# Products with the rows of v issued for four gathers at a time

## The reference, cut to what matters

```python
def peer_ffn(x, w_q, sub_keys, u_emb, v_emb):
    ...
    def chunk(xc):                                    # 128 tokens
        q = (xc @ w_q).reshape(PEER_CHUNK, PEER_HEADS, 2, PEER_HALF)
        s = jnp.einsum('thid,hikd->thik', q, sub_keys).astype(jnp.float32)
        ...                                           # the best 16 of 16384 experts per head: eidx, gate
        u = u_emb[eidx]
        hid = jax.nn.gelu(jnp.einsum('td,thkd->thk', xc, u))
        wgt = (gate * hid.astype(jnp.float32)).astype(xc.dtype)
        return jnp.einsum('thk,thkd->td', wgt, v_emb[eidx])
```

## Time and profile before

| | us |
|---|---|
| median of three runs | 4032.74 (4027.02 to 4035.24) |
| profiled execution, its own time | 4030.91 |
| its span | 4029.6 |
| PE busy in the span | 3244.0 (81%) |
| DVE busy | 1976.9 (49%) |
| POOL busy | 1526.5 (38%) |
| line 1854, products with v, 3072 records | 1067.8 |
| line 2025, gathers, 1536 issues | 1456.6 |
| gathers' share of the DMA engines' span | 50.9% |

### The profile page before, as it was taken

One profiled execution on the slowest core, in us unless ns is written; L12 is line 12 of the kernel. 1 busy time (PEld: TensorE's weight loads), 2 busy tenths in 40 slices (PEclk: granted clock), 3 DMA queues, 4 the chain that ended last, 5 costly groups with the idle time before them and its releaser, 6 DMA issues.

```text
span 4029.6 us, 28457 instructions
## 1 busy us (share of the span) xinstructions
PE 3244.0 (81%) x10226; PEld 1353.4 (34%) x10226; DVE 1976.9 (49%) x4445; ACT 376.2 (9%) x923; POOL 1526.5 (38%) x1577
## 2 busy tenths in 40 slices
PE   7989978777898877788878888878666666788898
PEld 3464334622452222522222222344511111134444
DVE  0041034776776663766666623134777677414122
ACT  1000031111000000000000000032000000012112
POOL 0010000364665564376666641000377777700000
PEclk9999989878999998899999999999888899899999
DMA  4134333797999998799999985311899999952222
GB/s 190 63 126 154 150 122 125 309 346 276 394 412 405 409 394 324 304 412 411 411 412 411 412 338 229 147 65 66 327 402 409 409 408 397 409 204 84 106 104 94
DMA packets 257129, 1125.38 MB, mean 279 GB/s; under 512 B 29552, under 2 KB 34672, under 8 KB 237788
## 3 DMA queue, kind: packets, MB, share of 16 engines
q0 software_dynamic: 221184, 805.40, 50.9%
q1 hardware_dynamic: 32380, 312.82, 19.9%
q10 hardware_dynamic: 3424, 5.34, 0.4%
HBM read 1117.06 MB, written 6.40 MB: 279 GB/s over the span
## 4 chain that ended last, share of the span: by engine, by line
PE 47%; DMA 25%; DVE 14%; POOL 7%; issue 4%; ACT 2%; SPq 0%; DVEq 0%; ACTq 0%
PE ps L228 15%; DMA big<-in_u,xT 15%; DMA big<-in_v,xT 7%; POOL big L2025 7%; PE ps L1854 5%; DVE big L1994 5%; PE ps L587 4%; PE ps L342 4%; PE ps L1793 4%; PE ps L1294 2%; PE ps L1330 2%; DMA w<-in_w_in 1%; PE ps L599 1%; PE ps L527 1%; PE ps L749 1%
## 5 line engine op out<-in xcount | busy, mean ns | idle before, releaser
L1854 PE MATMUL ps<-big,bc 128*32 128x512 f32 x3072 | 1067.8, 668 | 336.6 <-DMA big<-in_v,xT 324.0
L1994 DVE CUSTOM_DVE_ANT_0 big<-big,ps 128x1024 f32<-128x1024 f32 x768 | 926.3, 1215 | 423.7 <-DMA big<-in_u,xT 420.1
L2025 POOL DMA_INDIRECT big<-in_u,xT x768 | 729.0, 949 | 625.8 <-issue 166.6
L2025 POOL DMA_INDIRECT big<-in_v,xT x768 | 727.6, 947 | 278.7 <-issue 186.5
L228 PE MATMUL ps<-w,xT 128*128 128x512 f32 x1408 | 613.0, 597 | 18.6 <-DMA w<-in_w_in 10.0
L1854 PEld LDWEIGHTS ps<-big,bc 128*32 128x32 f32 x3072 | 193.2, 115 | 1093.8 <-DMA big<-in_v,xT 727.6
L228 PEld LDWEIGHTS ps<-w,xT 128*128 128x128 f32 x1408 | 268.8, 192 | 357.3 <-issue 344.6
L467 POOL TENSOR_TENSOR small<-small 128x32 f32<-128x32 f32 (+1 forms) x8 | 33.2, 4154 | 480.1 <-DVE small L438 329.8
L342 PE MATMUL ps<-w,small 128*2 128x512 f32 x384 | 180.5, 626 | 41.3 <-DMA w<-in_w_mod 40.7
L587 PE MATMUL ps<-w,xT 128*128 128x512 f32 x384 | 173.0, 610 | 17.3 <-DMA w<-in_w_in 15.6
L876 POOL TENSOR_TENSOR small<-small 128x8 f32<-128x8 f32 x4 | 6.5, 1634 | 448.7 <-DVE small L867 448.7
(11 more groups left out here) (295 smaller groups left out, 3006.7 us busy)
## 6 DMA issues: line engine op xcount, KB each, us to landing
w<-in_w_in SPq DMA_DIRECT2D x58, 2048.0 KB, 7.7
w<-in_w_mod SPq DMA_DIRECT2D x24, 2048.0 KB, 7.4
w<-in_w_conv SPq DMA_DIRECT2D x24, 1536.0 KB, 9.2
w<-in_peer_wq SPq DMA_DIRECT2D x12, 2048.0 KB, 10.4
w<-in_w_out SPq DMA_DIRECT2D x10, 2048.0 KB, 8.1
w<-in_conv_out_w SPq DMA_DIRECT2D x6, 2048.0 KB, 9.3
big<-in_u,xT POOLq DMA_INDIRECT x768, 10.3
big<-in_v,xT POOLq DMA_INDIRECT x768, 10.8
```

The lines of the kernel that those rows point to most:

```text
L1854: ins = pe.e.matmul(self.ps[32 * g:32 * g + 32, 2 + half, :], p["diag"][part % 2][:, 256 * g + 32 * m:256 * g + 32 * m + 32], p["ring"][:, ...
L1994: dve.inc(dve.e.tensor_tensor_reduce(out=row, in0=row, in1=p["xc"], scale=1.0, scalar=0.0, op0=ALU.mult, op1=ALU.add, accum_out=p["hid"][t ...
L2025: ins = pool.e.indirect_dma_start(p["ring"][:, slot, :], None, table, bass.IndirectOffsetOnAxis(index, 0))
```

## The change

PE no longer issues the products at every second v place but at every fourth, for four rows and all four column groups: first half, four groups; second half, four groups. There is one signal `sum` for four rows, and all who wait for it count in fours. The number of matmuls, their operands and the sums in PSUM are the same.

```diff
--- before.py
+++ after.py
@@ -1844,17 +1844,16 @@
                 pe.wait_ge(self.dve, name, "diag", part)
                 if part == 4:
                     pe.wait_ge(self.dve, name, "summed", 0)
-            if n % 2:
-                m, slots = n // 4, [ring["v", e - 1 + j] for j in range(2)]
+            if n % 4 == 3:
+                m, slots = n // 4, [ring["v", e - 3 + g] for g in range(4)]
                 for half in range(2):
-                    for j in range(2):
+                    for g in range(4):
                         if not half:
-                            pe.wait_ge(self.gathered[slots[j]], name, "v", e - 1 + j)
-                        g = n % 4 - 1 + j
+                            pe.wait_ge(self.gathered[slots[g]], name, "v", e - 3 + g)
                         ins = pe.e.matmul(self.ps[32 * g:32 * g + 32, 2 + half, :], p["diag"][part % 2][:, 256 * g + 32 * m:256 * g + 32 * m + 32],
-                                          p["ring"][:, slots[j], half * BANK:(half + 1) * BANK], start=part % 4 == 0 and m == 0,
+                                          p["ring"][:, slots[g], half * BANK:(half + 1) * BANK], start=part % 4 == 0 and m == 0,
                                           stop=part % 4 == 3 and m == 7)
-                pe.inc(ins, name, "sum", e // 2)
+                pe.inc(ins, name, "sum", e // 4)
 
     def peer_act(self, act, l, stream):
         name, p = f"peer{l}{stream}", self.peer_views()
@@ -1939,7 +1938,7 @@
 
         dve.wait_ge(self.pe, name, "weights turned", part)
         if part >= 2:
-            dve.wait_ge(self.pe, name, "sum", 16 * (part - 2) + 15)
+            dve.wait_ge(self.pe, name, "sum", 8 * (part - 2) + 7)
         shape = (P, 4, 8, 4)
         flat = p["diag"][part % 2]
         out = bass.AP(flat.tensor, flat.offset, [list(flat.ap[0]), [256, 4], [36, 8], [1, 4]])
@@ -1950,7 +1949,7 @@
 
         t = self.merged[:, tile, :]
         dve.wait_ge(self.row_in[0], "row", name, "gate")
-        dve.wait_ge(self.pe, name, "sum", 64 * tile + 63)
+        dve.wait_ge(self.pe, name, "sum", 32 * tile + 31)
         for half in range(2):
             c = slice(half * BANK, (half + 1) * BANK)
             dve.inc(dve.x.tensor_tensor(t[:, c], self.ps[:, 2 + half, :], self.bc[:, 0, c], ALU.mult))
@@ -2012,7 +2011,7 @@
                 if before == "u":
                     pool.wait_ge(self.dve, name, "dot", b)
                 else:
-                    pool.wait_ge(self.pe, name, "sum", b // 2)
+                    pool.wait_ge(self.pe, name, "sum", b // 4)
             if kind == "u":
                 if e % TOPK == 0:
                     pool.wait_ge(self.dve, name, "experts", e // TOPK)
```

## The result

The changed kernel takes 4150.0 us (median of four runs, 4147.5 to 4157.5); the kernel before took 4034.0 us in the same comparison. The ratio is 1.029, 95% interval 1.028 to 1.031: 116 us slower. The forecast, +20 us, had the direction and the stage and under a fifth of the size; its range ended at 4100 us.

A forecast was written before the change was run, and what follows sets the result against it. The prediction took transfers to bound the second and third stage and the ring of slots to cause POOL's waits in the first. It summed +31 - 8 - 3 = +20 us to 4053 us, range 4010 to 4100.

The forecast's parts named there:

- the sum for the turn of the ring of ten: First stage, 1000 to 1500 us: eight gathers take three issues 3.76, L, burst 1.91 and 0.28: 13.2 us, +31 us.
- L: Time from a gather's issue to its landing; taken as 7.3 us in the first stage, bounds 5.7 and 8.7.
- the cover from 800 to 1000 us: First stage: gathers come slower than the ring needs, so it costs nothing; shorter bursts give -8 us, bounds 0 and -15.
- What bounds the kernel before: Transfers pace the second and third stage; in the first, POOL's 167.6 us of waits for line 1854 are for the ring.
- that PE was the pace: Rival, first stage: POOL's waits are PE's load, so halving bursts pays about 18 us, 4015 us; chance 0.23.
- The cost of a burst: Products on PE: four column groups run together, so four rows cost 1.91 us instead of 3.82, 367 us less work.
- Three issues: Ring of 10: three gather issues by POOL between a release and the next group's last row, 3.76 us.
- The tail: Last 32 v rows of the first stage, without u between: 48 us become 41 at best; -3 us forecast.
- The ring of 16: Second and third stage: four rows at a time cost 0 us, up to +5 each if the cover is thin.
- The copy of the turned experts and the renumbered counts: DVE's waits before its copy shrink but its next product waits anyway, and counts wait for the same last rows: 0.
- Slower by more: Rival: groups go two and two, or PE stands at weights when a group lands; 44 us on top, 4097; chance 0.12.
- The bound of 88 us: First stage, 1000 to 1500 us: with L = 8.7 the ring costs 2.2 us in each of 40 turns.

The follow-up runs named there:

- pairs_late: Kernel before, products still in pairs, but POOL waits for the second pair of four before refilling any of the four slots: 4135.3 us, ratio 1.024.
- quads_r10_busy: quads_r10 plus three sets of added zero-matrix products per turn, sums unchanged: 4211.2 us, ratio 1.015 to the kernel before, which took 4148.4 us beside it.
- quads_warm2: Changed kernel plus zero-matrix products, as much as a pair's and at a pair's time, in all three stages: 4137.5 us, ratio 1.026 to the kernel before.
- quads_rest: Changed kernel with pairs in the first peer stage, four rows at a time only in the second and third: 4033.2 us, ratio 0.9995 to the kernel before.
- quads_r13: Kernel before with four rows at a time and 13 slots instead of 16 in the third stage: 4154.4 us, ratio 0.997; before took 4165.4 us there.
- quads_r10: Kernel before with four rows at a time and 10 slots instead of 16 in the third stage alone: 4223.7 us, ratio 1.046.
- pairs_r10: Kernel before, pairs kept, with 10 slots instead of 16 in the third stage: 4039.9 us, ratio 1.001.
- quads_r12b: Kernel before with four rows at a time and 12 slots instead of 16 in the third stage, at the usual bandwidth: 4059.3 us, ratio 1.006.
- quads_r10c: quads_r10 run again, as partner of quads_r10_busy: 4265.9 us, ratio 1.028 to the kernel before, which took 4148.4 us beside it.

## Why the prediction was wrong

The step that failed is the sum for the turn of the ring of ten, 5.95 + L with L = 7.3. Its form was right; two of its terms were too small, L (8.17 us measured) and the burst (2.80 instead of 1.91). The second failed step is the cover from 800 to 1000 us, where the ring was said to cost nothing and cost 35 us.

*What bounds the kernel before: right.* POOL's waits for line 1854 were waits for the ring. The likeliest rival, that PE was the pace, is refuted by pairs_late (PE's load as before, 99 us slower) and by the changed kernel itself (PE 81 us less busy, 116 us slower).

*The cost of a burst: right at full clock.* Sixteen records, four groups together:

```profile
1672.46 1.92 PE L1853 MATMUL ps<-big,bc 128*32 128x512 f32 x16
```

1.92 us, as a pair's eight took the earlier trace rows. The products' busy time fell by only 90 us all the same, where 192 x 1.91 = 367 were reckoned, as more groups run at the lower clock or in parts, row by row. The gain of only 2.38 for three column groups that the Trainium skill gives (TensorE: Matmul & The Clock Gate, "Measured speedup vs the span model") isn't what this kernel shows: four column groups take no longer here than two.

*The turn of the ring: the right form, and the step that failed.* The sum gave 13.2 us. Measured from 1000 to 1500 us over 34 turns: 0.28 + 3.94 + 8.17 + 2.80 = 15.2 us, mean turn 15.06. Against the four terms:
- L was taken from the medians of all gathers in a stretch. In the sum stands the mean, and of one row only, the last of its group, which is issued with up to seven others still under way: 8.17 us, though the median of these same rows is 6.5. Weight loads make some of them much longer, and a turn pays each in full: 9.7 us on average for 15 of these rows that have a load of weights beside them, up to 16.5, and 6.2 for the 11 that have none. +0.9 us. The median of all gathers in that stretch fell from 9.3 to 6.6 us, close to the 6.4 that the prediction named as the sign of its fastest rival, while the mean of the rows in the sum was above 8.
- The burst was taken at full clock and at the moment of landing, 1.91 us. It ends 2.80 us after the landing, with 33% of the records at the lower level (7% before). Of the 27 groups whose landing the trace has, 13 end 1.95 us after the landing, 12 run at the lower clock and take up to 3.67 us, and two find side work in the way. +0.9 us. The grouping isn't to blame: pairs_late has late bursts of the same kind, and a mean turn of 14.9 us. The lower clock was mentioned and weighed only for the third stage and for each stage's end, where it cost nothing; in the ring of ten it comes off no allowance and lengthens each turn in which it occurs, and quads_r10_busy shows a price for it.
- Three issues, 3.94 instead of 3.76. +0.2 us.

From place 160 to 480 (1055 to 1643 us, a little past that stretch) eight gathers grew from 12.6 to 14.7 us, 2.1 us in each of 40 turns: these are the +82 us, where 0.8 us and 31 us were forecast.

*800 to 1000 us: wrong in sign.* -8 us was forecast, as eight gathers took 16 us there and the ring asked for 5.95 + 5.7. Measured: +35 us, a turn of 17.2 us, of which 6.9 are L and 5.8 the time from landing to the burst's end, 77% of the records at the lower clock (37% before). I had set the ring's turn of an idle PE against the pace of the attention units as if the larger of the two would hold. They add up: PE is in order, the group waits behind an attention unit (in all six groups from 880 to 1000 us whose landing the trace has, work of line 1635, 1642 or 1649 stands between the landing and the burst's end), and POOL waits for the group. In the kernel before a pair's landing-to-end time was longer still, 8.7 us, but a pair's release frees slots sooner, and the ring hid a part of it. The late release alone costs 15 of the 35 us (pairs_late), and most of the rest goes when the clock is kept up (quads_warm2).

*The tail: right.* -3 us forecast, -5 measured. *The ring of 16: right*, +3.5 and 0 us, and quads_rest at 0.9995. *The copy of the turned experts and the renumbered counts:* nothing to be seen of them.

*The rivals and the range.* "Slower by more" named as its sign a group that ends 1 us or more later than its last row's landing plus 1.91. That came true in 10 of 27 groups from 1000 to 1500 us, but not for its reasons: the groups didn't go two and two, and what delayed them was the lower clock from 1000 to 1500 us and attention units before that. It expected L to end below the 7.3 us of the sum, where 8.17 was measured; its 44 us on top were for the burst alone, and it had a chance of 0.12. The bound of 88 us that L = 8.7 gave stood in the text and was left out of the range: in the prediction's own sum it gives 4033 + 88 - 8 - 3 = 4110 us, and with 0.9 us more for the burst in each of 40 turns 4146.

What stays open: how exactly the 17 us between pairs_late and the changed kernel divide between the clock and the grouping. The traces put them from place 32 to 160 (+20 us, less 5 in the tail), and quads_warm2 gives three quarters of the 20 back, but these are single traces, and the interval of quads_warm2 holds both readings. Why the third stage had less bandwidth in some of the experiments is open too. Nothing that was run beats the kernel before in both conditions: quads_r13 is 11 us under it where there was less bandwidth, and quads_rest, the same idea with 16 slots, equals it otherwise.

## What to carry to other kernels

A signal that is given for more work at once is also a later release: before batching consumers, count how many places of the ring stand between the first row's landing and the release, and add up the loop from release to release with the mean, not the median, of the flight time. A wait for an engine on a ring of buffers is not a sign that the engine is slow; it may be late because it was told to wait. And where a loop leaves TensorE idle, price its bursts at the lower clock as well: in quads_r10 three quarters of the product records ran there.

## What the runs showed that was not expected

- Ten slots carry pairs at 405 GB/s and fours at 308 GB/s (pairs_r10, quads_r10), and two slots more give fours 392 GB/s (quads_r12b).
- Adding products that change no sum made a kernel 55 us faster (quads_r10_busy against quads_r10c), as TensorE's granted clock rose from 0.73 to 0.89.
- The third stage ran at 364 to 366 GB/s in one set of experiments, even where the ring doesn't bind, and at 405 in another: the kernel before took 4165 and 4034 us beside them. The cause isn't known; the record has both 4034 and 4148 us for the kernel before under one chip number (quads_r10 and quads_r10c). A turn that binds in one condition may be hidden in the other.
